# The second statistic of a seam from sums taken before scaling, and seven residual adds on GpSimd during the next products

## Chip, cores and metric

One core of one Trainium2 chip. The metric is the device time of one execution in microseconds (us); lower is better. Three runs of the kernel before are given, and one further execution that was profiled.

## What is computed

The reference is a two-layer backbone over 512 latent tokens and 256 context tokens of width 1024, in float32. Each layer has three sub-layers: a SwiGLU feed-forward, a mixer (state-space heads beside Fourier heads), and another feed-forward. Around each of them stands the same frame:

```python
def _rmsnorm(x, g):
    y = xf * lax.rsqrt(jnp.mean(xf * xf, axis=-1, keepdims=True) + EPS)
    return (y * g.astype(jnp.float32)).astype(x.dtype)
def _pre(x, g, mod, k):
    return _rmsnorm(x, g) * (1.0 + mod[:, 3 * k + 1][:, None]) + mod[:, 3 * k][:, None]
def _post(x, y, g, mod, k, weight):
    return x + weight * mod[:, 3 * k + 2][:, None] * _rmsnorm(y, g)
```

So between two sub-layers the output y of one is normalised, scaled and added to x, and the new x is normalised again and becomes h, the input of the next. I call this stretch a seam. There are five seams between the six sub-layers, and a sixth at the end that only adds to x.

## The kernel before

**Layout.** Activations lie transposed in SBUF: 8 chunks (`KC`) of 128 features in the partitions, with `TOK` = 768 tokens along the row (256 context, 512 latent). `xT` is x, `yT` the output of the sub-layer, `hH` and `hL` the high and low parts of h. From the last mixer's output on only the 512 latent tokens are computed (`tok0` = 256). Each product is three TensorE passes (high by high, low by high, high by low) at L473, over 384 tokens each, or 512 where only latent tokens count. Weights arrive in units of 128x1024; `split_hi` (ScalarE) and `split_lo` (VectorE, L465) part them.

**Order.** Every engine runs one program written out by hand; waits are semaphores. Nothing reorders. Per section the calls are: the sub-layer (`ffn_*` or `mix_*`), then `post_*`, then the `pre_*` part of the next.

**End of a section.** The last eight output chunks are made one after another in `last_chunks` (TensorE), 24 passes each. `last_adds` (VectorE, L992, L1006, L1010) adds each into `yT`; ScalarE squares it into `sq`; GpSimd adds the squares of chunks 0 to 5 up into `sumY` (`add_squares`, L1265). The last two chunks are split in halves of 384 tokens.

**The seam.** TensorE sums `sumY` and the last squares over the features (`row_sums`, L1302); VectorE turns the sums into columns (L1310), ScalarE takes the root (L1376), VectorE the reciprocal (L1462), and TensorE spreads it over all partitions into PSUM (`spread_matmuls`, L1317). Then `post_vector` scales all eight chunks of y (L1471; y from SBUF, the spread row from PSUM). `POOL_CHUNKS`, 0 to 3, are added to x by GpSimd, the others by VectorE (both L1282). ScalarE squares each chunk of the new x (L1411), TensorE sums each (L1302) with filler products between (`keep_clock`, L1326), and the same turn, root, reciprocal and spread follow for x. `pre_vector` makes `tmpN` from x (L1496; x from SBUF, the row from PSUM), ScalarE adds the shift and rounds into `hH` (`add_shift`, L1423), and VectorE makes `hL` from `tmpN` and `hH` (L1500), both in SBUF. Two token ranges, 256 and 512 wide, make two instructions of each per chunk.

**The next section's start.** `first_groups` runs the first weight units together, chunk by chunk as h appears: chunks 0 to 4 for all units, then chunks 5 to 7 unit by unit. A feed-forward opens three units so, a mixer two. A mixer then interleaves projections 2 to 7 with `state_inputs` (L1702), and VectorE scans over the chunks of time (L2105, L2106) beside it; the scans of the first quarter stand behind the split of unit 7, which waits for projection 4. The tile `Tz`, which a DMA loads late in the mixer (waited for at L1764), comes behind the last scan. The mixers and the first feed-forward of each layer store x to DRAM and load it back (`spill_x`, `reload_x`) to use its space.

## Time and profile before

| | us |
|---|---|
| median of three runs | 2648.16 (2646.20 to 2650.08) |
| profiled execution | 2646.27 |
| its span, first to last instruction | 2644.5 |
| TensorE busy | 2586.2 |
| VectorE busy | 1596.0 |
| GpSimd busy | 816.1 |
| ScalarE busy | 714.7 |

The span is one execution; what lies around it is 1.8 us. Busy times overlap, so they do not add up. A seam is read in the chain of waits, which follows the work that ended last back through the engines: the rows below name at each step who was waited for. PE is TensorE, DVE VectorE, ACT ScalarE, POOL GpSimd. In a timeline, instructions of one kind that follow each other are merged; `x15` is their count.

### The profile page before, as it was taken

The page shows a single profiled execution, that of the slowest core. Times are in us where ns is not written, and L with a number is a line of the kernel's source. Part 1 is how long each engine was busy: PE and PEld are TensorE (multiplying, and loading weights), DVE is VectorE, ACT ScalarE, POOL GpSimd, SP SyncE. Part 2 cuts the span into 40 slices and gives each one's busy share as a digit, 9 for nine tenths or more (in the row PEclk, how much of TensorE's full clock was granted, in tenths as well). Part 3 has the DMA queues.
Part 4 walks back from the last instruction along what each step waited for, and adds up shares of the span by engine and source line. Part 5 has one row for each costly group of instructions (what it writes and reads, how often), then busy time and mean ns, then how long its engine had stood idle before and what let it go on. Part 6 is the DMA issues. An engine that isn't in the chain of part 4 may idle for free.

```text
span 2644.5 us, 40750 instructions
## 1 busy us (share of the span) xinstructions
PE 2586.2 (98%) x17044; PEld 2429.9 (92%) x17044; DVE 1596.0 (60%) x2238; ACT 714.7 (27%) x1050; POOL 816.1 (31%) x1286
## 2 busy tenths in 40 slices
PE   6999999999999999999999999999999999999998
PEld 5999999998989899999999899999999878888886
DVE  6688878766574676676676633433343684544443
ACT  4222212123334411212113412122122424322223
POOL 1278876832140100000001148667651131000001
PEclk9999999999999999999999999999999999999999
DMA  9534444453364234434432422222223565233331
GB/s 338 154 123 156 157 143 133 161 187 132 117 194 144 79 98 136 130 108 138 136 104 91 109 67 83 94 92 90 94 88 116 189 196 163 72 96 96 96 96 64
DMA packets 346831, 334.54 MB, mean 127 GB/s; under 512 B 52496, under 2 KB 319896, under 8 KB 343576
## 3 DMA queue, kind: packets, MB, share of 16 engines
q1 hardware_dynamic: 284344, 198.19, 25.7%
q10 hardware_dynamic: 52288, 77.20, 8.7%
q0 software_dynamic: 10016, 56.56, 5.6%
q8 instruction: 134, 2.20, 0.3%
q14 instruction: 49, 0.40, 0.0%
HBM read 287.40 MB, written 44.50 MB: 126 GB/s over the span
## 4 chain that ended last, share of the span: by engine, by line
PE 86%; DVE 8%; POOL 2%; issue 1%; ACT 1%; DMA 1%; SPq 0%; DVEq 0%; POOLq 0%; ACTq 0%
PE ps L473 81%; POOL xT L1282 1%; DVE tmpN L1496 1%; DVE hL L1500 1%; PE ps L1302 1%; PE ps L1317 1%; DVE zb L2105 1%; DVE zd L2106 1%; PE ps L1050 1%; ACT wH L458 1%; PE ps L1069 1%; DVE zc L2118 0%; PE ps L1326 0%; DVE SR L2122 0%; PE ps L1702 0%
## 5 line engine op out<-in xcount | busy, mean ns | idle before, releaser
L473 PE MATMUL ps<-hH,wH 128*128 128x384 f32 (+1 forms) x2928 | 1013.5, 346 | 8.5 <-DVE hL L1500 8.0
L473 PE MATMUL ps<-hH,wL 128*128 128x384 f32 (+1 forms) x2928 | 1004.9, 343 | 0.0
L473 PE MATMUL ps<-hL,wH 128*128 128x384 f32 (+1 forms) x2928 | 1004.5, 343 | 0.0
L465 DVE TENSOR_TENSOR wL<-raw,wH 128x1024 fp32r<-128x1024 f32 x300 | 396.4, 1332 | 493.2 <-ACT wH L458 491.7
L473 PEld LDWEIGHTS ps<-hH,wH 128*128 128x128 f32 x2928 | 549.9, 188 | 35.4 <-DVE hL L1500 7.4
L473 PEld LDWEIGHTS ps<-hH,wL 128*128 128x128 f32 x2928 | 550.1, 188 | 18.1
L473 PEld LDWEIGHTS ps<-hL,wH 128*128 128x128 f32 x2928 | 550.2, 188 | 17.8
L473 PE MATMUL ps<-midH,wH 128*128 128x384 f32 (+1 forms) x1232 | 424.0, 344 | 2.9 <-DVE yT L948 2.5
L473 PE MATMUL ps<-midH,wL 128*128 128x384 f32 (+1 forms) x1232 | 421.5, 342 | 0.0
L473 PE MATMUL ps<-midL,wH 128*128 128x384 f32 (+1 forms) x1232 | 421.3, 342 | 0.0
L458 ACT ACTIVATE wH<-raw 128x1024 fp32r<-128x1024 f32 x300 | 310.9, 1049 | 366.2 <-PE ps L473 349.5
L1265 POOL TENSOR_TENSOR sumY<-sq 128x768 f32<-128x768 f32 (+1 forms) x6 | 10.0, 1659 | 1039.7 <-ACT sq L1384 1039.7
L584 DVE SCALAR_TENSOR_TENSOR adaW<-adaW,siluC 128x384 f32<-128x384 f32 x520 | 329.0, 684 | 0.8
L926 DVE TENSOR_TENSOR midF<-ps,sgate 128x768 f32<-128x768 f32 (+1 forms) x88 | 78.4, 890 | 318.1 <-PE ps L473 317.9
L948 DVE TENSOR_TENSOR yT<-ps,yT 128x768 f32<-128x768 f32 (+1 forms) x256 | 223.2, 885 | 71.3 <-PE ps L473 71.3
L473 PEld LDWEIGHTS ps<-midH,wH 128*128 128x128 f32 x1232 | 231.3, 188 | 13.4 <-DVE yT L948 5.3
L473 PEld LDWEIGHTS ps<-midL,wH 128*128 128x128 f32 x1232 | 231.4, 188 | 6.8
L473 PEld LDWEIGHTS ps<-midH,wL 128*128 128x128 f32 x1232 | 231.3, 188 | 6.8
L882 ACT ACTIVATE midH<-midF 128x768 fp32r<-128x768 f32 (+1 forms) x88 | 69.8, 793 | 575.0 <-DVE midF L926 575.0
L875 ACT ACTIVATE sgate<-ps 128x768 f32<-128x768 f32 (+1 forms) x88 | 66.9, 760 | 216.7 <-PE ps L473 206.1
L930 DVE TENSOR_TENSOR midL<-midF,midH 128x768 fp32r<-128x768 f32 (+1 forms) x88 | 81.8, 930 | 0.0
L666 ACT ACTIVATE modraw<-ps 128x3 f32<-128x3 f32 x76 | 9.1, 172 | 240.7 <-PE ps L473 240.7
(284 smaller groups left out, 2261.3 us busy)
## 6 DMA issues: line engine op xcount, KB each, us to landing
raw<-in_ffn_gu_dram SPq DMA_DIRECT2D x176, 512.0 KB, 3.9
adaW<-in_w_ada_dram ACTq DMA_DIRECT2D x40, 1536.0 KB, 7.0
raw<-in_ffn_down_dram SPq DMA_DIRECT2D x88, 512.0 KB, 3.5
x_d<-xT POOLq DMA_DIRECT2D x4, 3072.0 KB, 11.2
xT<-x_d POOLq DMA_DIRECT2D x4, 3072.0 KB, 10.6
ada_early<-in_w_ada_dram POOLq DMA_DIRECT2D x6, 1536.0 KB, 18.7
W_d<-gW POOLq DMA_DIRECT2D x16, 512.0 KB, 3.8
VT_d<-gVT ACTq DMA_DIRECT2D x16, 512.0 KB, 3.0
```

The source lines that it names most:

```text
L458: nc.scalar.activation(wH[:, n % SPLIT_SLOTS, :], raw[:, n % RAW_SLOTS, :], ACT.Copy).then_inc(w_hi, 1)
L465: nc.vector.tensor_tensor(wL[:, n % SPLIT_SLOTS, :], raw[:, n % RAW_SLOTS, :], wH[:, n % SPLIT_SLOTS, :].bitcast(f32), ALU.subtract).then_ ...
L473: ins = nc.tensor.matmul(dst, a, b, start=first and n == 0, stop=last and n == 3 * len(pairs) - 1)
L584: ins = stt(at, w[:, k], siluC[:, k, v:v + 1], adaP[:] if i == 3 else at, ALU.mult, ALU.add)
L875: nc.scalar.activation(sb_pair(sgate[:, f % 2, :], F.tok0), ps_pair(tile_slot(F, g), F.tok0), ACT.Silu)\
L882: nc.scalar.activation(midH[:, f % 4, F.tok0:TOK], midF[:, f % 2, F.tok0:TOK], ACT.Copy).then_inc(mid_hi, 1)
L926: nc.vector.tensor_tensor(sb_pair(midF[:, f % 2, :], F.tok0), ps_pair(tile_slot(F, g), F.tok0), sb_pair(sgate[:, f % 2, :], F.tok0), ALU.m ...
L930: nc.vector.tensor_tensor(midL[:, f % 4, F.tok0:TOK], midF[:, f % 2, F.tok0:TOK], midH[:, f % 4, F.tok0:TOK].bitcast(f32), ALU.subtract).t ...
L948: ins = nc.vector.tensor_tensor(sb_pair(yT[:, m, :], F.tok0), ps_pair(tile_slot(F, g + m), F.tok0), sb_pair(yT[:, m, :], F.tok0), ALU.add)
L1050: ins = nc.tensor.transpose(ps[:, 6 + a, t * 128:(t + 1) * 128], gV[:, a, t, :], ident[:])
L1069: ins = nc.tensor.matmul(ps[32 * p:32 * p + 32, 6 + g2, c0:c1], Bw[half, a, dd, p, :], rhs(half, a, dd, p), start=first, stop=last)
L1282: engine.tensor_tensor(xT[:, m, N.tok0:TOK], xT[:, m, N.tok0:TOK], yT[:, m, N.tok0:TOK], ALU.add)\
```

## The change

Write z for `coefP`*y, the output times its gate and gain, and r for the reciprocal root of y's mean square. The new x is x + r*z, so its sum of squares is that of the old x, plus 2r times the sum of x*z, plus r^2 times the sum of z^2. The change takes the second statistic from these:

- **Sums of squares per chunk.** `add_squares` is skipped for the five seams with a successor. Instead `square_sums` puts each `sq` chunk through TensorE in `last_chunks`, with `statP` as weights: one column of ones and two of `coefP` squared, so that one pass gives y's sum and those of z for latent and context.
- **Sums of x*z.** `cross_z` (VectorE, in `last_adds`) multiplies yT, `coefP` and xT, chunk by chunk. With 768 tokens chunks 0 to 5 are added up on VectorE, and three row sums are taken behind the last squares; with 512 tokens each chunk has its row sum. x must be back in SBUF by then (`wait_back` moves ahead).
- **The statistic.** `new_sums` (VectorE) has it in five small instructions; a running `sumX` holds the sum of squares of x. `square_x` and the eight row sums of the seam go, with the fillers between.
- **Adds to x.** VectorE adds chunk 0, GpSimd chunks 1 to 7, in the seams with a successor. Before the last output GpSimd keeps four.
- **The seam's order on VectorE.** `joined_vector` scales chunk m+2 of y between `tmpN` and `hL` of chunk m. ScalarE copies the spread row from PSUM to `rowY` in SBUF; chunk 0 is scaled with the row in PSUM, chunks 1 to 7 with `rowY`.
- **Starts.** A mixer opens three units, its state inputs stand one projection later, and the head weights `CW` are made in other banks.

VectorE at the second seam (first mixer to second feed-forward), before: from the last scaling of y to the first low part of h.

```order
L1471 SCALAR_TENSOR_TENSOR yT<-yT,coefP,ps 128x512
L1282 TENSOR_TENSOR xT<-xT,yT 128x768 x4
L465 TENSOR_TENSOR wL<-raw,wH 128x1024
L1310 TENSOR_REDUCE rstdX<-ps 128x6
L1487 RECIPROCAL rstdX<-rstdX 128x6
L1496 SCALAR_TENSOR_TENSOR tmpN<-xT,coefA,ps 128x256
L1496 SCALAR_TENSOR_TENSOR tmpN<-xT,coefA,ps 128x512
L1500 SCALAR_TENSOR_TENSOR hL<-tmpN,coefS,hH 128x256
L1496 SCALAR_TENSOR_TENSOR tmpN<-xT,coefA,ps 128x256
L1500 SCALAR_TENSOR_TENSOR hL<-tmpN,coefS,hH 128x512
```

The same place in the changed kernel, from the scaling of chunk 0 on.

```order
L1582 SCALAR_TENSOR_TENSOR yT<-yT,coefP,ps 128x512
L1632 RECIPROCAL rstdX<-rstdX 128x6
L1347 TENSOR_TENSOR xT<-xT,yT 128x768
L1582 SCALAR_TENSOR_TENSOR yT<-yT,coefP,rowY 128x256
L1582 SCALAR_TENSOR_TENSOR yT<-yT,coefP,rowY 128x512
L1637 SCALAR_TENSOR_TENSOR tmpN<-xT,coefA,ps 128x256
L1637 SCALAR_TENSOR_TENSOR tmpN<-xT,coefA,ps 128x512
L1641 SCALAR_TENSOR_TENSOR hL<-tmpN,coefS,hH 128x256
L1582 SCALAR_TENSOR_TENSOR yT<-yT,coefP,rowY 128x256
L1582 SCALAR_TENSOR_TENSOR yT<-yT,coefP,rowY 128x512
L1641 SCALAR_TENSOR_TENSOR hL<-tmpN,coefS,hH 128x512
L475 TENSOR_TENSOR wL<-raw,wH 128x1024
```

The scalings of chunks 1 to 7 moved from before the second statistic to between `tmpN` and `hL`, and read `rowY`; three of the four adds to x left VectorE.

TensorE at the same seam, before: from the mixer's last product to the first sums over the new x.

```order
L473 MATMUL ps<-hH,wL 128x384
L1302 MATMUL ps<-sumY,ones 32x192 x4
L1302 MATMUL ps<-sq,ones 32x96 x16
L1326 MATMUL ps<-ident 128x128 x3
L1317 MATMUL ps<-ident,rstd 128x128 x6
L1326 MATMUL ps<-ident 128x128 x13
L1302 MATMUL ps<-sq,ones 32x192 x4
L1326 MATMUL ps<-ident 128x128 x3
```

And in the changed kernel, to the next section's first product.

```order
L483 MATMUL ps<-hH,wL 128x384
L1372 MATMUL ps<-sq,statP 32x192 x4
L1372 MATMUL ps<-sq,statP 32x96 x16
L1372 MATMUL ps<-xzM_95,ones 32x192 x4
L1372 MATMUL ps<-xzM_96,ones 32x192 x8
L1388 MATMUL ps<-ident,rstd 128x128 x6
L1397 MATMUL ps<-ident 128x128 x2
L1388 MATMUL ps<-ident,rstdX 128x128 x6
L1397 MATMUL ps<-ident 128x128 x7
L483 MATMUL ps<-hH,wH 128x384
```

The two spreads now follow each other with only fillers between. Not shown: five further row sums of 32x192 stand between the products of the section's last chunks.

```diff
-    def first_groups(pe, base, count, pre, between=None):
-
-        pe.wait_ge(w_lo, base + count)
+    def first_groups(pe, base, count, pre, between=None, cw_ready=None):
+
         lead = KC - 3
         order = [(k, u) for k in range(lead) for u in range(count)]
         order += [(k, u) for u in range(count) for k in range(lead, KC)]
         for k, u in order:
             if u == 0:
                 pe.wait_ge(h_lo, KC * pre.nth + k + 1)
+            if k == 0:
+                pe.wait_ge(w_lo, base + u + 1)
+                if u == 1 and cw_ready:
+                    pe.wait_ge(cw, cw_ready)
+                if u == 2:
+                    pe.wait_ge(row_y, pre.after.nth + 1)
...
+    def cross_sums(pe, S, m):
+
+        pe.wait_ge(cross_x, cross_count(S, m))
+        return row_sums(pe, 6, crossed(S, m), S.tok0, TOK, m == 0, m == KC - 1)
+
+    def square_sums(pe, S, m, t0, t1, first=False, last=False):
+
+        return row_sums(pe, 7, sq[:, m, :], t0, t1, first, last, statP[:, m, :])
...
             signal(last_part(pe, S, m, moving, range(HC), (0, 1)), m)
+            while S.next and m >= 2 and summed < m:
+                pe.wait_ge(sq_y, KC * S.post.nth + summed + 1)
+                square_sums(pe, S, summed, S.tok0, TOK, summed == 0)
+                if S.tok0:
+                    cross_sums(pe, S, summed)
+                summed += 1
...
         if S.next:
             coef_pre(dve, S.next)
+            wait_back(dve, S.post)
+            dlink(dve, nc.vector.memset(statP[:], 1.0))
+            dsync(dve)
+            dlink(dve, nc.vector.tensor_tensor(statP[:, :, 1:3], coefP[:], coefP[:], ALU.mult))
...
             nc.vector.tensor_tensor(at, ps_pair(last_slot(S, m), S.tok0), at, ALU.add).then_inc(S.read, 1)
+            if S.next:
+                dve.wait_ge(S.read, S.read0 + m + 1)
+                ins = cross_z(dve, S, m, token_segments(S.tok0))
+                if S.tok0:
+                    ins.then_inc(cross_x, 1)
+                else:
+                    dlink(dve, ins)
+                    if m:
+                        dsync(dve)
+                        ins = nc.vector.tensor_tensor(crossed(S, 0), crossed(S, 0), crossed(S, m), ALU.add)
+                        if m < CROSS_SUMMED - 1:
+                            dlink(dve, ins)
+                        else:
+                            ins.then_inc(cross_x, 1)
...
-    def add_squares(pool, N):
-
+    def add_squares(pool, N, S):
+
+        if S.next:
+            return
...
-    def post_pool(pool, N):
+    def post_pool(pool, N, S):
         wait_back(pool, N)
-        for m in POOL_CHUNKS:
+        if not N.has_next:
+            for m in range(LAST_POOL):
+                pool.wait_ge(y_norm, KC * N.nth + m + 1)
+                add_to_x(pool, nc.gpsimd, N, m, x_new)
+            return
+        for m in range(1, KC):
             pool.wait_ge(y_norm, KC * N.nth + m + 1)
-            add_to_x(pool, nc.gpsimd, N, m, x_new_pool)
-
-    def row_sums(pe, bank, squares, t0, t1, first, last):
+            add_to_x(pool, nc.gpsimd, N, m, x_new)
...
+            ins = square_sums(pe, S, m, N.tok0 or HALF, TOK, False, m == KC - 1)
+        ins.then_inc(ss_y, 1)
+        for m in range(KC - 3, KC) if N.tok0 else (0, KC - 2, KC - 1):
+            ins = cross_sums(pe, S, m)
+        ins.then_inc(ss_x, 1)
+        pe.wait_ge(rs_y, N.nth + 1)
+        spread_matmuls(pe, 4, 5, N.tok0, rstd, bc_y, bc_y_ctx)
+        keep_clock(pe, 2)
...
+        if S.next:
+            root(act, rstdX[:], sumX[:], N.tok0, sum_x, N.nth + 1, sd_x)
+            act.wait_ge(y_norm, KC * N.nth + 1)
+            for t0, t1, v in token_segments(N.tok0):
+                ins = nc.scalar.activation(rowY[:, t0:t1], seg_ps(4, 5, v), ACT.Copy)
+            ins.then_inc(row_y, 1)
...
+    def scale_y(dve, N, m):
+        for t0, t1, v in token_segments(N.tok0):
+            if m == 0 and v == LAT:
+                dve.wait_ge(bc_y, N.nth + 1)
+            row = seg_ps(4, 5, v) if m == 0 and N.has_next else rowY[:, t0:t1] if N.has_next else seg_ps(2, 3, v)
+            ins = nc.vector.scalar_tensor_tensor(yT[:, m, t0:t1], yT[:, m, t0:t1], coefP[:, m, v:v + 1], row,
+                                                 ALU.mult, ALU.mult)
+        ins.then_inc(y_norm, 1)
+
+    def new_sums(dve, N, S):
+
+        b = N.tok0 // 128
+        r, d, c, x = (t[:, b:6] for t in (rstd, sumD, cross, sumX))
+        dve.wait_ge(rs_y, N.nth + 1)
+        for b0, b1, v in [(b, 2, CTXV), (2, 6, LAT)][b // 2:]:
+            dlink(dve, nc.vector.tensor_tensor(sumD[:, b0:b1], turnedY[:, b0:b1, 1 + v], rstd[:, b0:b1], ALU.mult))
+        dve.wait_ge(ss_x, N.nth + 2)
+        columns(dve, 6, N.tok0, cross).then_inc(cols_x, 1)
+        dve.wait_ge(cols_x, N.nth + 2)
+        dsync(dve)
+        dlink(dve, nc.vector.scalar_tensor_tensor(d, c, 2.0, d, ALU.mult, ALU.add))
+        dsync(dve)
+        dlink(dve, nc.vector.tensor_tensor(d, d, r, ALU.mult))
+        dsync(dve)
+        dlink(dve, nc.vector.tensor_tensor(x, x, d, ALU.add))
+        dsync(dve)
+        nc.vector.tensor_scalar(x, x, 0.0, None, ALU.max).then_inc(sum_x, 1)
...
+    def joined_vector(dve, post, N, late):
+
+        if N.tok0 == 0:
+            dve.wait_ge(bc_y_ctx, post.ctx_nth + 1)
+        dsync(dve)
+        scale_y(dve, post, 0)
+        inverse_x(dve, N)
+        dve.wait_ge(y_norm, KC * post.nth + 1)
+        add_to_x(dve, nc.vector, post, 0, x_new)
+        dve.wait_ge(row_y, post.nth + 1)
+        scale_y(dve, post, 1)
+        dve.wait_ge(bc_x if N.tok0 else bc_x_ctx, N.nth + 1)
+        for m in range(KC):
             if m >= 2:
                 dve.wait_ge(h_lo, KC * N.nth + m - 1)
+            wait_x(dve, post, m)
             for t0, t1, v in token_segments(N.tok0):
-                ins = scaled(m, t0, t1, v)
+                if m == 0 and v == LAT:
+                    dve.wait_ge(bc_x, N.nth + 1)
+                ins = scaled(N, m, t0, t1, v)
+                if m == 0 and v == CTXV:
+                    ins.then_inc(h_tmp_ctx, 1)
             ins.then_inc(h_tmp, 1)
-            if m >= 1:
-                rest(m - 1)
-        rest(KC - 1)
+            if m == 0 and N.tok0 == 0:
+                c, l = token_segments(0)
+                dve.wait_ge(h_hi_ctx, N.nth + 1)
+                low(0, *c)
+                scale_y(dve, post, 2)
+                dve.wait_ge(h_hi, KC * N.nth + 1)
+                low(0, *l).then_inc(h_lo, 1)
+            elif m + 2 < KC:
+                scale_y(dve, post, m + 2)
+                rest(dve, N, m)
+            elif m == KC - 1:
+                rest(dve, N, m - 1)
+                rest(dve, N, m)
+            if m == 0:
+                for n in late:
+                    split_lo(dve, n)
...
-        first_groups(pe, M.base, 2, pre)
+        first_groups(pe, M.base, 3, pre, None, M.gen.n0["cw"] + 1)
```

## Rows read from the trace of the kernel before

**Rows 1.** the page, span and part 1, whole execution: busy us, share, instructions

```profile
...
span 2644.5 us, 40750 instructions
...
PE 2586.2 (98%) x17044; PEld 2429.9 (92%) x17044; DVE 1596.0 (60%) x2238; ACT 714.7 (27%) x1050; POOL 816.1 (31%) x1286
...
```

**Rows 2.** the chain of waits, second seam: start us, us, engine, tile, line

```profile
...
876.15 0.02 issue
...
880.42 0.76 DVE yT L1471
...
881.31 7.16 POOL xT L1282 x4
...
894.30 0.20 DVE rstdX L1487
...
894.55 1.62 PE ps L1317 x12
...
898.63 26.43 PE ps L473 x151
...
```

**Rows 3.** the chain of waits, first seam (two rows), fifth seam (two rows)

```profile
...
635.16 0.02 issue
...
685.77 2.79 PE ps L1702 x64
...
2243.24 0.02 issue
...
2262.26 27.94 PE ps L473 x122
...
```

**Rows 4.** timeline, second seam, VectorE and ScalarE: start us, us, instructions xcount

```profile
...
880.42 8.10 DVE L1471 SCALAR_TENSOR_TENSOR yT<-yT,coefP,ps 128x512 f32<-128x512 f32 x15 [0.41 <-PE ps L1317]
888.43 3.55 DVE L1282 TENSOR_TENSOR xT<-xT,yT 128x768 f32<-128x768 f32 x4
891.90 1.22 DVE L465 TENSOR_TENSOR wL<-raw,wH 128x1024 fp32r<-128x1024 f32 x1
...
903.75 1.14 DVE L1496 SCALAR_TENSOR_TENSOR tmpN<-xT,coefA,ps 128x256 f32<-128x256 f32 x2
904.81 1.14 DVE L1500 SCALAR_TENSOR_TENSOR hL<-tmpN,coefS,hH 128x256 fp32r<-128x256 f32 x2
...
902.69 1.13 ACT L1423 ACTIVATE hH<-tmpN,coefS 128x256 fp32r<-128x256 f32 x2 [1.34 <-DVE tmpN L1496]
...
```

**Rows 5.** timeline, GpSimd and VectorE together; one line's durations, ns, min/median/max

```profile
...
853.13 1.84 POOL L1265 TENSOR_TENSOR sumY<-sq 128x768 f32<-128x768 f32 x1 [46.52 <-ACT sq L1384]
...
854.02 2.03 DVE L465 TENSOR_TENSOR wL<-raw,wH 128x1024 fp32r<-128x1024 f32 x1 [1.86 <-ACT wH L458]
...
L584 DVE SCALAR_TENSOR_TENSOR adaW<-adaW,siluC x520: 602/611/1647, 73.5 to 1417.7; 128x384 f32<-128x384 f32 x174
...
303.01 7.36 DVE L584 SCALAR_TENSOR_TENSOR adaW<-adaW,siluC 128x384 f32<-128x384 f32 x5
...
```

**Rows 6.** TensorE's waits, first mixer and second mixer: us in total, times, longest

```profile
...
PE ps L1764 <- DMA Tz<-strip_d: 0.6, 1, 0.6
...
PE ps L1764 <- DMA Tz<-strip_d: 1.7, 1, 1.7
...
```

**Rows 7.** timeline, TensorE, row sums at the first and the fifth seam

```profile
...
635.08 0.53 PE L1302 MATMUL ps<-sumY,ones 128*32 128x192 f32 x8
635.42 0.68 PE L1302 MATMUL ps<-sq,ones 128*32 128x96 f32 x24
...
2250.46 0.42 PE L1302 MATMUL ps<-sq,ones 128*32 128x128 f32 x8
2250.82 0.94 PE L1326 MATMUL ps<-ident 128*128 128x128 f32 x6
...
```

**Rows 8.** busy us of each engine in two stretches; PEclk is the granted clock

```profile
...
2142.46:2145.07 2.61, 0.01 (x2) 0.03 (x1) 2.58 (x3) 0.24 (x2) 1.32 (x1) 1.00 0.99 377
2145.67:2149.08 3.41, 3.41 (x6) 1.35 (x5) 3.34 (x6) 0.00 (x0) 0.00 (x0) 0.50 1.18 225
...
```

More of the change, by code:

```diff
@@ L1477, in post_vector @@
-        for n in S.late[:1]:
-            split_lo(dve, n)
+        if S.next:
+            new_sums(dve, N, S)
+        else:
+            wait_back(dve, N)
+            dsync(dve)
+            for m in range(KC):
+                scale_y(dve, N, m)
+            for m in range(LAST_POOL, KC):
+                dve.wait_ge(y_norm, KC * N.nth + m + 1)
+                add_to_x(dve, nc.vector, N, m, x_last)
     def flip_rows(dve, N):
         dve.wait_ge(ss_x, N.nth + 1)
-        columns(dve, N.banks[0], N.tok0, rstdX).then_inc(cols_x, 1)
+        columns(dve, N.banks[0], N.tok0, sumX).then_inc(cols_x, 1)
@@ new lines, in scaled, with low, rest @@
+    def scaled(N, m, t0, t1, v):
+        return nc.vector.scalar_tensor_tensor(tmpN[:, m % 2, t0:t1], xT[:, m, t0:t1], coefA[:, m, v:v + 1],
+                                              seg_ps(*N.banks, v), ALU.mult, ALU.mult)
+    def low(m, t0, t1, v):
+        return nc.vector.scalar_tensor_tensor(hL[:, m, t0:t1], tmpN[:, m % 2, t0:t1], coefS[:, m, v:v + 1],
+                                              hH[:, m, t0:t1].bitcast(f32), ALU.add, ALU.subtract)
+    def rest(dve, N, m):
+        dve.wait_ge(h_hi, KC * N.nth + m + 1)
+        for t0, t1, v in token_segments(N.tok0):
+            ins = low(m, t0, t1, v)
+        ins.then_inc(h_lo, 1)
@@ new lines, in first_vector @@
+    def first_vector(dve, N):
+        dve.wait_ge(bc_x_ctx, N.nth + 1)
+        dsync(dve)
+        c, l = token_segments(0)
+        scaled(N, 0, *c).then_inc(h_tmp_ctx, 1)
+        dve.wait_ge(bc_x, N.nth + 1)
+        scaled(N, 0, *l).then_inc(h_tmp, 1)
+        dve.wait_ge(h_hi_ctx, N.nth + 1)
+        low(0, *c)
+        scaled(N, 1, *c)
+        dve.wait_ge(h_hi, KC * N.nth + 1)
+        low(0, *l).then_inc(h_lo, 1)
+        scaled(N, 1, *l).then_inc(h_tmp, 1)
+        for m in range(2, KC):
+            if m in LATE_COEFS:
@@ L1777, in outputs @@
             ins.then_inc(y_ps, 1)
-        for m in range(2, 8):
+        for m in range(3, 8):
             proj(m)
-            if m >= 2 and m < 6:
-                state_inputs(m - 2)
+            if m < 7:
+                state_inputs(m - 3)
         channels(0)
```

214 lines of the change are left out of this document (113 added, 101 removed).

## The prediction

> **What bounds the kernel now.** The page first [rows 1]: TensorE is busy for 98% of the span, and nearly all of it is products at L473, whose number does not change. So only two things can move the time: instructions added to TensorE's stream while it is full, and the stretches at the seams where it has no products. Then the chain of waits through the second seam [rows 2]. The last product ends at 876.15, which I call T. The first product of the next section starts at 898.63, T+22.5. Between lie the first statistic, the scaling of chunk 0 (done at T+5.0), 7.16 us of GpSimd adding four chunks to x, the squares and sums of the second statistic, the second spread of 1.62 us, and the first chunk of h. From 898.63 TensorE is continuous: it has three weight units open, so a chunk of h feeds it for 18 products of 0.175 us (26.43 us over 151), 3.15 us, while VectorE makes a chunk in 2.2. The 24 groups of six end at T+22.5+24 x 1.05 = T+47.7. That moment, three units done over all eight chunks, is what I compare; call it E.
>
> The first seam is the other kind [rows 3]: only two units are open, TensorE follows VectorE, and the third unit is done at 685.77, E = T+50.6; the fourth seam has the same 50.6. The fifth has 512 tokens: products start at T+19.0, a group costs 3 x 0.229 = 0.69, E = T+35.5. The sixth seam keeps its way. Five seams change.
>
> **The change: the seam's head.** The second statistic no longer needs the new x, so GpSimd's 7.16 us and eight squares and sums leave the chain. The start stays: chunk 0 scaled at T+5.0; the three sums of x*z (about 0.4 us each on TensorE, below) lie beside the root and the reciprocal, and the small VectorE operations end before the spread does. I take T+5.1. Then, on VectorE: a reciprocal 0.2, chunk 0 into x 0.9 [rows 4], chunk 1 scaled 1.07: T+7.4; the second spread (1.62 after the reciprocal [rows 2]) is ready by T+7.0, hidden. tmpN of chunk 0 takes 1.14 [rows 4]: T+8.5. So far so good; without anything else the first h would stand near T+10.7.
>
> **The step that decides: GpSimd's adds beside VectorE.** Before, GpSimd's adds ran beside L1471, which reads one operand from PSUM: four adds at 1.79 each while VectorE kept 0.54 per instruction (8.10 over 15) [rows 2, 4]. Nothing waited. Now seven adds run beside instructions that read both operands from SBUF: the scaling of chunks 1 to 7, whose row is now rowY, and hL, from tmpN and hH. What such a pair does is seen where it occurs [rows 5]: L465 begins at 854.02, GpSimd's instruction ends at 854.97, and L465 ends 1.08 after that: 2.03 in place of 1.22. L584, the same kind of instruction as hL, takes 0.61 alone and 7.36 for five in a row beside GpSimd, 1.47 each, one whole GpSimd instruction per VectorE instruction. So the two take turns, an instruction at a time, and I charge each add fully to VectorE unless it falls beside tmpN, which reads PSUM.
>
> Does it fall there? The add of chunk m+2 is released when scaling of m+2 ends. On VectorE the next instructions are the two of hL(m), and only behind them tmpN(m+1). hL waits for ScalarE's 1.13 [rows 4], so GpSimd asks at that very moment, and gets its turn before hL or between its halves. Nothing of it falls beside tmpN. A chunk then costs tmpN 1.14 + scaling 1.08 (two of the 0.54) + hL 1.06 (1.14, begun 0.08 early, row 904.81) + the add 1.82 (row 853.13) = 5.10 us, against 3.15 of TensorE's work.
>
> The Trainium skill, page "SBUF — State Buffer", section "Who interferes with whom", says that a VectorE instruction with two SBUF inputs and a GpSimd instruction that reads SBUF exclude each other for a whole instruction; by it the seams come out at the sum below, without it at that of rival (a). It speaks against the change.
>
> Working it through: the add of chunk 1 (T+7.5 to 9.35) holds back the first half of hL(0); with 0.4, the scaling of chunk 2 1.07 and the second half 0.67, chunk 0 of h is ready at T+11.5. Queued next is one weight split (1.22) behind the add of chunk 2: chunk 1 is ready at 11.5 + 1.82 + 1.22 + 1.14 + 1.07 + 1.07 + 1.82 = T+19.6. Chunks 2 to 5: 4 x 5.10, T+40.0. Chunks 6 and 7 have nothing left to scale: 2 x 2.21, T+44.4. TensorE still owes seven groups then (the units finish one after another over the last three chunks): 0.14 + 7 x 1.05. E = T+51.9.
>
> Against before: second and third seam +4.2 each. First and fourth, where three units are now open: +1.3. But in the first mixer TensorE waits 0.6 for Tz, in the second 1.7 [rows 6], at the end of VectorE's scans; those start from projection 4, ahead of which one block of state inputs less stands now (2.79 [rows 3]), so the scans come 1.5 earlier and the waits absorb: +0.7 and -0.4. Fifth seam, adds of 1.2 to 1.3 (estimate from 1.82 by size), a chunk 3 x 0.67 + 1.28 = 3.3: E between T+32.5 and T+35.8, I take -0.5. **Seams: +8.2.**
>
> **The sections' ends.** While the last eight output chunks run, TensorE is full, and the change puts the sums of squares in there one chunk at a time; the GpSimd additions that it drops there cost nothing (they only made L465 wait, 2.03 against 1.22, with TensorE busy). A row sum of 192 columns is 0.34 from start to start (635.08 to 635.42), its busy time 0.53; one of 128 columns 0.36 with its neighbours [rows 7]. With four interruptions a section I take 0.4 and 0.3: four sections x 5 x 0.4 = 8.0, and the second mixer, which also sums x*z there, 10 x 0.3 = 3.0. **+11.0**, bounds 9 and 14. The new VectorE passes (x*z, and adding it up: about two per chunk of 1 us) lie under 24 x 0.175 = 4.2 us of products per chunk, beside one add and half a split: 3.6 in all. They are free; if the last one slips past T, 0.5 per seam. Moving the head weights costs nothing: ScalarE has time during the stall.
>
> **TensorE's clock.** In the second mixer a gap of 2.61 us was followed by 3.41 us at half clock, 1.2 GHz [rows 8]; gaps up to 1.7 had none. The new seam has gaps of some 5 us between chunks 0 and 1 and of 2 between the others. A slow stretch where TensorE waits anyway costs nothing; on the last seven groups it costs up to 1.7. Bounds 0 and 5 x 1.7; I take one, +1.7. The Trainium skill, page "TensorE: Matmul & The Clock Gate", section "What's actually happening", has the clock fall when the engine has been idle and return with activity; by it each long gap has such a stretch, and the sum would be nearer the upper bound.
>
> Sum: 8.2 + 11.0 + 1.7 = 20.9. The profiled execution took 2646.27 (span 2644.5), the median of the runs is 2648.16, 1.9 more: 2646.3 + 20.9 + 1.9 = **2669 us**.
>
> **Rivals.** (a) The other sign: GpSimd's adds and VectorE's SBUF pairs run side by side after all. A chunk is 3.28, near TensorE's 3.15; chunk 7 is ready at T+32.7, E = T+40.1: -7.6 at two seams, about -11 and -12 at the mixers, -8 at the fifth: -46 + 11 = -35, 2613. It decides from the point where an add costs VectorE under 0.3 us a chunk. For it: L1471 ran undisturbed. Against: [rows 5]. (b) The turns fall kindly: both halves of hL go first and the add lies under tmpN, so that only 0.7 of it is lost. A chunk is 4.0, E = T+46: -17 + 11, 2642; faster or the same by a hair. Against: GpSimd always got the turn after the instruction running. (c) All as forecast, and each seam ends in a slow stretch (4 x 1.7 more) while the row sums reach their bound (+3): 2679. (d) The waits in the mixers do not shrink: +2.3, inside the range, counted with the forecast.
>
> **Numbers.** Forecast 0.57, (a) 0.13, (b) 0.15, (c) 0.15. The range 2638 to 2688 leaves out (a) and a little above (c). About 0.2%, 5.3 us, is what a measurement of this kernel tells from no change. Faster 0.18 (all of (a), a third of (b)), same 0.11 (the rest of (b), a little of the forecast), slower 0.71.
>
> **What the profile would show.** Right: hL and the scaling with rowY near or above 1.1 to 2.5 us an instruction where GpSimd runs, a period near 5.1 us per chunk in the seam, h of chunk 0 near T+11.5 and TensorE idle for about 2 us a chunk, E near T+52. Row sums in the sections' ends lengthening these by about 2 us. Wrong: hL at its 1.07 per chunk throughout, or TensorE continuous after its first new product.

## The result

| | median us | lowest to highest | profiled: time, span |
|---|---|---|---|
| before | 2649.12 | 2646.2 to 2656.12 | 2646.27, 2644.5 |
| changed | 2680.09 | 2676.75 to 2683.55 | 2676.75, 2674.9 |

The changed kernel is slower: a ratio of 1.0112, 95% interval 1.0094 to 1.0130. The forecast was 2669, range 2638 to 2688; the sum was +20.9 and the two profiled spans differ by 30.5 (unrounded). The direction and its main cause came out as predicted; the terms for the sections' ends, the clock and the two mixers were too small.

The page of the changed kernel, span and part 1, against [rows 1]. TensorE executes fewer instructions and idles more; VectorE is busier by 93 us.

```profile
span 2674.9 us, 40386 instructions
...
PE 2568.9 (96%) x16804; PEld 2410.6 (90%) x16804; DVE 1688.7 (63%) x2362; ACT 687.6 (26%) x1019; POOL 800.3 (30%) x1276
```

The chain of waits through the second seam, where T is 883.29 (start us, us, what; against [rows 2]).

```profile
887.16 1.17 DVE yT L1582 x2
...
904.35 0.04 DVE hL L1641
904.38 1.95 issue
906.33 0.74 DVE hL L1641
...
925.37 14.67 PE ps L483 x74
```

Before, TensorE was the chain from T+22.5 on. Now the first product starts at T+11.2, but VectorE stays on the chain until T+42.1, because chunk after chunk stands 1.95 us inside the first of its two hL instructions, in a stretch for which the profile names nobody ("issue"). What happens in those 1.95 us stands in the timeline, VectorE first, then GpSimd (start us, us, then x and the count of instructions).

```profile
903.08 1.14 DVE L1582 SCALAR_TENSOR_TENSOR yT<-yT,coefP,rowY 128x256 f32<-128x256 f32 x2
904.35 2.72 DVE L1641 SCALAR_TENSOR_TENSOR hL<-tmpN,coefS,hH 128x256 fp32r<-128x256 f32 x2
...
904.30 1.83 POOL L1347 TENSOR_TENSOR xT<-xT,yT 128x768 f32<-128x768 f32 x1 [3.13 <-DVE yT L1582]
```

The add into x starts at 904.30, hL at 904.35, and the pair that took 1.14 before [rows 4] takes 2.72. TensorE's longest wait by line, over the whole span (us in total, times, longest), is the one for hL in front of its products:

```profile
PE ps L483 <- DVE hL L1641: 56.6, 33, 3.6
```

The next table says where the 30.5 us are, by the distance from one section's last product to the next; T1 to T5 are the last products ahead of the five seams that change. A section's "end" is the time of the last 192 products before T (96 in the second mixer). E, as in the prediction, is when three weight units are done over all eight chunks, counted from the T in front of it.

| | longer by | of it the section's end | the rest | E before, changed |
|---|---|---|---|---|
| start to T1 | 2.6 | 3.0 | -0.4 | |
| T1 to T2 (first mixer) | 4.5 | 3.1 | +1.5 | 50.6, 52.2 |
| T2 to T3 | 7.6 | 3.1 | +4.5 | 47.7, 52.2 |
| T3 to T4 | 7.5 | 3.1 | +4.4 | 47.7, 52.2 |
| T4 to T5 (second mixer) | 7.8 | 3.8 | +4.0 | 50.6, 52.3 |
| T5 to the end | 0.4 | | +0.4 | 35.7, 35.3 |

So 16.1 us lie in the ends and 14.4 in the seams and what follows them. Ratios below are to the kernel before, with their 95% interval; the changed kernel's is the 1.0112 above. The kernel before was run again beside each group of experiments, with medians from 2649 to 2655, so small steps are better read from the ratios than from the medians.

### The profile page after: what moved, and what is told of

Read it like the earlier page. It is cut to its first block, busy times and chain, and to the rows that moved or that the text cites. A ratio compares the mean times of both kernels' runs of the same rounds, so it can differ in the third digit from the quotient of the medians.

```text
span 2674.9 us, 40386 instructions
## 1 busy us (share of the span) xinstructions
PE 2568.9 (96%) x16804; PEld 2410.6 (90%) x16804; DVE 1688.7 (63%) x2362; ACT 687.6 (26%) x1019; POOL 800.3 (30%) x1276
## 4 chain that ended last, share of the span: by engine, by line
PE 80%; DVE 11%; issue 3%; ACT 2%; DMA 1%; POOL 1%; SPq 1%; DVEq 0%; ACTq 0%; POOLq 0%
PE ps L483 77%; DVE tmpN L1637 1%; DVE hL L1641 1%; DVE yT L1582 1%; ACT hH L1543 1%; DVE wL L475 1%; PE ps L1372 1%; DVE zb L2282 1%; DVE zd L2283 1%; POOL xT L1347 1%; PE ps L1111 1%; SPq L1754 1%; PE ps L1130 1%; ACT wH L468 0%; DVE zc L2295 0%
## 5 line engine op out<-in xcount | busy, mean ns | idle before, releaser
L1347 POOL TENSOR_TENSOR xT<-xT,yT 128x768 f32<-128x768 f32 (+1 forms) x39 | 67.1, 1724 | 910.1 <-DVE yT L1582 910.1
L1641 DVE SCALAR_TENSOR_TENSOR hL<-tmpN,coefS,hH 128x256 fp32r<-128x256 f32 (+1 forms) x88 | 91.4, 1074 | 4.2
## 6 DMA issues: line engine op xcount, KB each, us to landing
xT<-x_d POOLq DMA_DIRECT2D x4, 3072.0 KB, 11.5
```

The costliest lines, as they stand in the source:

```text
L1347: engine.tensor_tensor(xT[:, m, N.tok0:TOK], xT[:, m, N.tok0:TOK], yT[:, m, N.tok0:TOK], ALU.add)\
L1641: return nc.vector.scalar_tensor_tensor(hL[:, m, t0:t1], tmpN[:, m % 2, t0:t1], coefS[:, m, v:v + 1], hH[:, m, t0:t1].bitcast(f32), ALU.ad ...
```

## Experiments

### The adds on VectorE, and no adds

```diff
     def post_pool(pool, N, S):
...
-        for m in range(1, KC):
-            pool.wait_ge(y_norm, KC * N.nth + m + 1)
-            add_to_x(pool, nc.gpsimd, N, m, x_new)
     def joined_vector(dve, post, N, late):
...
+            if m + 1 < KC:
+                dve.wait_ge(y_norm, KC * post.nth + m + 2)
+                add_to_x(dve, nc.vector, post, m + 1, x_new)
```

> The changed kernel, with the seven additions into x of each seam on VectorE (behind hL of the chunk before) and none on GpSimd. Theory (the two engines take turns, and an add costs VectorE its whole 1.8 us): a chunk becomes tmpN 1.14 + scaling 1.08 + hL 1.1 + add 0.96 = 4.3 us in place of 4.95, chunk 0 of h is ready 0.4 earlier, and E (three units done over all chunks) falls from T+52.1 to about T+46; over four seams about -20 us, so 2658 to 2662. Rival (GpSimd does not hold VectorE back, and the period of 4.95 comes from VectorE's own instructions with two SBUF operands): every chunk gets 0.96 longer, a period near 5.9, E near T+58, and the kernel is some 20 us slower than the changed one, near 2700.

Measured: 2672.49 us, ratio 1.0074 (1.0057 to 1.0091). The rival falls: the kernel became faster than the changed one, not 20 us slower. But the gain is 10 by the ratios (8 by the medians), not 20. The second kernel leaves out the adds into x of chunks 1 to 7, so it gives a price and is no candidate.

> The changed kernel without the additions into x of chunks 1 to 7 of the five seams (that part of the computation is left out; chunk 0 is still added). It prices them. Theory (turns): hL takes its 1.1 us and the period falls from 4.95 to 3.3, near TensorE's 3.15; chunk 0 of h is ready near T+10.7, E near T+40; four seams by 12 and some 2 at the fifth, less what waits for Tz and for state inputs give back in the mixers: 2680 - 40 = 2640, and 2630 to 2655 as bounds. Rival (a mere part of the 4.95 is the adds, the rest ScalarE's hH on the way): the period stays above 4, E above T+46, 2660 or more.

Measured: 2635.18 us, ratio 0.9935 (0.9919 to 0.9951). The timelines of VectorE, first without adds, then with the adds on VectorE:

```profile
1466.90 1.15 DVE L1640 SCALAR_TENSOR_TENSOR hL<-tmpN,coefS,hH 128x256 fp32r<-128x256 f32 x2
1467.96 1.13 DVE L1636 SCALAR_TENSOR_TENSOR tmpN<-xT,coefA,ps 128x256 f32<-128x256 f32 x2
...
1471.36 1.13 DVE L1636 SCALAR_TENSOR_TENSOR tmpN<-xT,coefA,ps 128x256 f32<-128x256 f32 x2
```

```profile
908.70 1.15 DVE L1638 SCALAR_TENSOR_TENSOR hL<-tmpN,coefS,hH 128x256 fp32r<-128x256 f32 x2
909.77 0.95 DVE L1347 TENSOR_TENSOR xT<-xT,yT 128x768 f32<-128x768 f32 x1
```

Without adds the forecast held (2640, period 3.3, E T+40): hL is back at 1.15 and a chunk takes 3.39 (1467.96 to 1471.36); E falls to T+40.4 in two seams and T+42.0 in the others. In the changed kernel a chunk takes 4.95, so one add of 1.80 on GpSimd costs VectorE 1.56. On VectorE itself it costs 0.95 and 0.1 until tmpN follows: 4.45 per chunk, half a microsecond less than 4.95, where I had expected 4.3. E falls to T+48.9 (49.7 at the first seam), not 46, and the two full seams give 3.3 each. The first mixer, however, became 5.2 us longer from T to T, although its E came 2.6 earlier. TensorE's waits there, which were 0.2 and nothing in the changed kernel:

```profile
PE ps L1944 <- DMA Tz<-strip_d: 3.0, 1, 3.0
PE ps L1882 <- ACT ZI L2105: 2.1, 1, 2.1
```

Neither wait is for an instruction of VectorE; they pointed at the queue of the next experiment. The spans differ by 1.9 only, but this profiled execution was the longest of its four (2674.76), and its first mixer had a further slow stretch of TensorE's clock, so the median says more.

### SyncE's queue in the mixers

```diff
-        load_units(RAW_SLOTS, 5)
+        load_units(RAW_SLOTS, 6)
         sp.wait_ge(h_lo, KC * pre.nth + KC)
         load_phases(1)
+        load_units(6, 7)
         load_chunks(0)
+        load_units(7, 8)
         load_chunks(1)
-        load_units(5, 7)
...
-        load_units(7, 8)
```

> The changed kernel with SyncE's queue in the mixers in another order: the loads of weight units 5, 6 and 7 stand ahead of the loads of the projected chunks 0, 0 and 1 instead of behind chunk 1 and behind the first state inputs. Theory (in the changed kernel these loads wait in the queue behind loads that wait for projections and state inputs one projection later than before, so ScalarE waits 14.7 us for them in the second mixer and comes late to the state inputs): ScalarE's wait falls to some 3 us, TensorE's wait of 2.5 us for the state inputs' buffer goes, and the second mixer gets 2.5 to 4 us shorter, the first 0 to 1.5: 2680 - 4 = 2676. Rival (the wait comes from the state inputs themselves standing one projection later, with the loads beside the path): ScalarE's wait may shrink but TensorE's 2.5 us stay, no change within 0.1%.

Measured: 2674.10 us, ratio 1.0082 (1.0066 to 1.0098); 2676 was expected. The interval still touches that of the changed kernel (1.0094 to 1.0130), so the evidence is in the traces. The second mixer, T to T, is 3.8 shorter (201.8 against 205.6); the first is 1.4 shorter, as much as its E came earlier (T+50.9). The changed kernel's chain of waits there shows the cause: SyncE issues the small loads of the projected chunks one at a time, 0.43 and 0.04 each, sixteen in a row (2121.11 to 2128.82), and the weights behind them arrive late, so that ScalarE reaches the state inputs (ZI) late.

```profile
...
2128.39 0.43 SPq L1754
2128.82 0.04 issue
2128.87 4.41 DMA raw<-in_w_in_dram
...
2137.31 1.75 ACT ZI L2105 x6
```

SyncE's timeline in the same mixer, changed kernel, then the experiment (T is the same within 0.1): the loads of units 5 and 6 went out at T+61.2 (T+50.7 in the kernel before) and that of unit 7 at T+69.0; now unit 5 stands ahead of this stretch, unit 6 goes at T+50.0 and unit 7 at T+56.2.

```profile
2128.87 1.06 SPq L459 DMA_DIRECT2D raw<-in_w_in_dram  x2
...
2136.66 0.56 SPq L459 DMA_DIRECT2D raw<-in_w_in_dram  x1
```

```profile
2117.58 0.37 SPq L459 DMA_DIRECT2D raw<-in_w_in_dram  x1
...
2123.78 0.49 SPq L459 DMA_DIRECT2D raw<-in_w_in_dram  x1
```

And TensorE's waits over that mixer, changed kernel and experiment. The wait for ZI is gone, and most of the one for Tz.

```profile
PE ps L1927 <- DMA ctxCS<-in_dft_ctx_dram: 2.6, 1, 2.6
PE ps L1882 <- ACT ZI L2105: 2.5, 1, 2.5
PE ps L1944 <- DMA Tz<-strip_d: 1.5, 1, 1.5
```

```profile
PE ps L1927 <- DMA ctxCS<-in_dft_ctx_dram: 2.6, 1, 2.6
...
PE ps L1944 <- DMA Tz<-strip_d: 0.4, 1, 0.4
```

### The row sums behind the last product

```diff
             signal(last_part(pe, S, m, moving, range(HC), (0, 1)), m)
-            while S.next and m >= 2 and summed < m:
-                pe.wait_ge(sq_y, KC * S.post.nth + summed + 1)
-                square_sums(pe, S, summed, S.tok0, TOK, summed == 0)
-                if S.tok0:
-                    cross_sums(pe, S, summed)
-                summed += 1
...
-        square_sums(pe, S, KC - 3, N.tok0, TOK)
+        for m in range(KC - 2):
+            square_sums(pe, S, m, N.tok0, TOK, m == 0)
```

> The changed kernel with the row sums of squares of chunks 0 to 4 (and in the second mixer those of x*z) behind the section's last product instead of between the last chunks' products. Theory (a row sum costs 0.61 us there because it interrupts the stream of products; side by side they cost 0.34 each): the last 192 products take 33.9 us again in place of 37, 3.1 less in each of four sections and 3.8 in the second mixer; behind T five more sums of 0.34 stand ahead of the last squares, where 0.25 us was idle, +1.45 in each seam. Net -1.6 in four sections and about -2.4 in the fifth: -9, 2671. Rival (0.61 is the price of the row sum itself wherever it stands): +2.8 behind T against -3.1 before it, about -2 in all, 2678.

Measured: 2673.01 us, ratio 1.0077 (1.0060 to 1.0093), 9 us below the changed kernel by the ratios and 7 by the medians; 9 was expected. The ends are back at 33.9, 34.2, 33.8, 33.4 and 22.0, within 0.05 of before, and the first product comes only 1.16 later. So the row sums are all that had made the ends longer. The profiled span fell by 3.7 only: the experiment's TensorE spent more time at the lower clock (granted clock 0.986 in all four executions, 0.988 to 0.991 in the changed kernel), among it a stretch of 10.2 us late in the second mixer that the changed kernel's trace does not have. In the changed kernel, two row sums together between products, and one alone (TensorE's timeline):

```profile
859.35 0.86 PE L1372 MATMUL ps<-sq,statP 128*32 128x192 f32 x16
860.14 0.44 PE L483 MATMUL ps<-hH,wH 128*128 128x384 f32 x1
...
864.23 0.34 PE L483 MATMUL ps<-hH,wL 128*128 128x384 f32 x1
864.50 0.53 PE L1372 MATMUL ps<-sq,statP 128*32 128x192 f32 x8
864.96 0.45 PE L483 MATMUL ps<-hH,wH 128*128 128x384 f32 x1
865.25 0.34 PE L483 MATMUL ps<-hL,wH 128*128 128x384 f32 x1
```

Products start 0.17 apart. With one row sum between them it is 0.73, and 0.29 to the next product in place of 0.17: 0.67 in all. A second row sum beside the first adds 0.33 (0.79 from 859.35 to 860.14, against 0.46 from 864.50 to 864.96). So 0.33 is the row sum itself, and about as much, 0.34, goes into the change from products to row sums and back. Four such changes and five row sums are 3.0; measured 3.06, or 0.61 per row sum. Behind T, in the experiment (the next row is the sums of x*z), and the place in the changed kernel where TensorE waits for the last squares:

```profile
881.95 2.82 PE L1365 MATMUL ps<-sq,statP 128*32 128x192 f32 x80
884.59 1.16 PE L1365 MATMUL ps<-xzM,ones 128*32 128x192 f32 x24
```

```profile
884.50 0.37 PE L1372 MATMUL ps<-sq,statP 128*32 128x96 f32 x8 [0.25 <-ACT sq L1515]
```

The sums of x*z begin 2.57 after T (882.02) and began 1.40 after T in the changed kernel, 1.17 for five row sums. They take 5 x 0.33 = 1.65 there, and some 0.5 of it falls into the wait for the last squares, so 0.23 each is what they add behind T and not what a row sum costs. The price of the change is that of another shape of product: the products are 128*128 and the row sums 128*32, and eight products of another kind but the same shape, in the stream of the changed kernel, cost nothing beyond their own 0.11 each (two products that start 0.17 apart stand 0.97 apart around them, and 0.26 to the next: 0.88 for the eight).

```profile
342.38 1.04 PE L1111 MATMUL ps<-ident,gV 128*128 128x128 f32 x8
```

The Trainium skill, page "TensorEngine Tiling (Array Packing)", section "Key Properties", says that a change of tiling mode drains TensorE; the rows agree, with 0.34 for the change there and back.

### Another order on VectorE

```diff
-            elif m + 2 < KC:
-                scale_y(dve, post, m + 2)
-                rest(dve, N, m)
...
+        for m in range(1, KC):
+            if m + 1 < KC:
+                product(m + 1)
+            rest(dve, N, m)
+            if m + 3 < KC:
+                scale_y(dve, post, m + 3)
```

`product` is the two `scaled` of a chunk (tmpN) with their waits, `rest` is hL.

> The changed kernel with another order on VectorE in the seam: behind the scaling of chunk m+3 now comes tmpN of chunk m+2, which reads PSUM, and only then hL of chunk m+1; nothing else moves, GpSimd still adds. Theory (an add costs VectorE only what of it does not lie beside an instruction with a PSUM operand): of the 1.80 of an add 1.1 lie beside tmpN and 0.7 hold hL back, so a chunk takes 3.39 (the period without adds) + 0.7 = 4.1 in place of 4.95; E at the second and third seam T+47 to T+48 in place of T+52.1, the mixers gain less because SyncE's queue holds their weight loads back: 2680 - 12 = 2668, bounds 2662 and 2673. Rival (the price of an add is the same 1.56 wherever it lies, by load on the memory rather than by turns): period 4.95 again, E T+52, 2680.

Measured: 2652.58 us, ratio 1.0000 (0.9989 to 1.0011), below the expected bound of 2662: the whole loss of the change is undone by the order of three instructions. GpSimd's add now starts under tmpN:

```profile
1481.04 1.13 DVE L1637 SCALAR_TENSOR_TENSOR tmpN<-xT,coefA,ps 128x256 f32<-128x256 f32 x2
1482.09 1.90 DVE L1641 SCALAR_TENSOR_TENSOR hL<-tmpN,coefS,hH 128x256 fp32r<-128x256 f32 x2
...
1484.97 1.13 DVE L1637 SCALAR_TENSOR_TENSOR tmpN<-xT,coefA,ps 128x256 f32<-128x256 f32 x2
...
1481.20 1.84 POOL L1347 TENSOR_TENSOR xT<-xT,yT 128x768 f32<-128x768 f32 x1 [2.08 <-DVE yT L1582]
```

The add is as long as ever, tmpN is not touched (1.13), hL loses 0.75 in place of 1.56, and a chunk takes 3.93. E is T+45.6 (44.5 at the second seam). The gain is 28 by the medians and 30 by the ratios, more than twice the 12 that I had expected. Per section: -7.7 and -6.6 behind the two full seams, -3.2 and -3.3 in the mixers, -3.6 behind the fifth. E came 2 us earlier than worked out, as a chunk took 3.93, not 4.1, and no slow stretch of TensorE's clock lay on the last groups any more; and I had counted nothing for the fifth seam. The mixers still waited for ZI, 1.9 and 4.8 us: SyncE's queue again.

### The row in PSUM, and all together

For the scaling of all chunks the row stays in PSUM, and GpSimd's add is released by an hL, so that it runs beside the scaling and tmpN. Not shown are the new order on VectorE and the later start of the third weight unit, which the expectation describes.

```diff
-            row = seg_ps(4, 5, v) if m == 0 and N.has_next else rowY[:, t0:t1] if N.has_next else seg_ps(2, 3, v)
+            row = seg_ps(4, 5, v) if N.has_next else seg_ps(2, 3, v)
...
         for m in range(1, KC):
             pool.wait_ge(y_norm, KC * N.nth + m + 1)
+            if m >= 2:
+                pool.wait_ge(h_lo, KC * S.next.nth + m - 1)
```

> The changed kernel with the row of the scaling left in PSUM for all chunks, the order scaling (chunk m+3), tmpN (m+1), hL (m), and GpSimd's add of chunk m+2 released by hL of chunk m-1, so that it runs beside scaling and tmpN, which both read PSUM; the third weight unit waits for the last scaling (its banks) and makes up its first five chunks then. Theory (turns): hL takes 1.15 a chunk again and nothing is held back, period 3.4 as without adds; the third unit starts near T+28, E T+42 to T+44; in the mixers SyncE's queue takes back what goes beyond T+49: near 2680 - 2 x 9 - 2 x 3 = 2656, bounds 2648 and 2668. Rival (the price of an add does not depend on where its neighbour's operand lies): period 4.95, the third unit starts near T+36, E near T+52, 2680.

Measured: 2669.19 us, ratio 1.0062 (1.0041 to 1.0082). The mechanism held and the kernel did not: I had released the add one hL too late, and tmpN waited for it, a period of 4.29 and E at T+47.7 to T+48.9. The next kernel puts the row in PSUM, the row sums behind T and the reordered queue together.

```profile
1486.20 1.14 DVE L1638 SCALAR_TENSOR_TENSOR tmpN<-xT,coefA,ps 128x256 f32<-128x256 f32 x2 [1.02 <-POOL xT L1350]
1487.26 1.14 DVE L1642 SCALAR_TENSOR_TENSOR hL<-tmpN,coefS,hH 128x256 fp32r<-128x256 f32 x2
```

> The changed kernel with the PSUM row and its order, the row sums behind the last product, and SyncE's weight loads ahead of the chunks' loads in the mixers, together. If the three causes are separate and add up: seams E T+43 to T+45 (1.2 later for the row sums) against 52.1, four times, is -32; sections' ends -3.1 x 4 - 3.8 = -16; the second mixer's state inputs -3: 2680 - 48 = 2632, bounds 2625 and 2645, under the kernel before by 0.6%. If the mixers stay bound by SyncE's queue instead, their E does not count, and it comes out 10 to 14 later, near 2645, no different from the kernel before.

Measured: 2647.92 us, ratio 0.9983 (0.9973 to 0.9994), above the upper bound of 2645, with the late release still in it (E T+48.9, 50.0 at the second seam). Against the PSUM row alone that is -21 us by medians: the two mixers, T to T, came to 239.8 and 194.9 against 245.5 and 205.3 (their ends' 3.1 and 3.8 among it). With `if m >= 3: ... m - 2` in the release:

> The kernel with the three changes together, its GpSimd adds released one hL earlier (by hL of chunk m-3). In the run with all three an add was released so late that VectorE waited 0.9 for it in every chunk, a period of 4.29 with hL at 1.15. Theory (turns, adds free beside instructions with a PSUM operand): period 3.4, E near T+44 (it was T+48.9), the third unit from T+28 on, 5 us off at each of four seams, of which the mixers keep at least half: 2647 - 15 = 2632, bounds 2626 and 2638. Rival (an add costs something even beside PSUM operands, 0.5 or more a chunk): period 3.9 or more, E T+47, 2640 or more.

Measured: 2630.00 us, ratio 0.9926 (0.9909 to 0.9943). VectorE and GpSimd in the third seam:

```profile
1469.49 1.13 DVE L1577 SCALAR_TENSOR_TENSOR yT<-yT,coefP,ps 128x256 f32<-128x256 f32 x2
1470.54 1.13 DVE L1632 SCALAR_TENSOR_TENSOR tmpN<-xT,coefA,ps 128x256 f32<-128x256 f32 x2
1471.59 1.14 DVE L1636 SCALAR_TENSOR_TENSOR hL<-tmpN,coefS,hH 128x256 fp32r<-128x256 f32 x2
1472.64 1.13 DVE L1577 SCALAR_TENSOR_TENSOR yT<-yT,coefP,ps 128x256 f32<-128x256 f32 x2
...
1469.71 1.83 POOL L1343 TENSOR_TENSOR xT<-xT,yT 128x768 f32<-128x768 f32 x1 [4.38 <-DVE hL L1636]
```

An add of 1.83 stands beside two pairs with a PSUM operand, and none of them, nor hL behind them, is longer than alone. A chunk takes 3.15 (1469.49 to 1472.64). The rival, that an add costs something everywhere, falls. E was T+46.4 all the same, not T+44; the next section says why. The last kernel of this group has the other order with `rowY` in place of the PSUM row, again with the row sums behind T and the reordered queue.

> The changed kernel with the other order on VectorE (tmpN behind the scaling), the row sums behind the last product, and SyncE's weight loads ahead in the mixers. The order alone measured E T+45.6, ratio 1.000, and kept waits of 1.9 and 4.8 for the state inputs' buffer in the mixers, which the earlier loads should take away (they did with the changed kernel's order); the row sums alone gave 9. If they add up: 2652.5 - 6.7 - 9 = 2637, bounds 2631 and 2643, a ratio near 0.994 to the kernel before. If the mixers' waits come from something other than the queue: 2643.

Measured: 2633.33 us, ratio 0.9936 (0.9921 to 0.9951), 4 us better than expected. The mixers' waits of 1.9 and 4.8 for ZI are gone, as the queue theory wants.

### What bounds E now

With the PSUM row TensorE stood 5.4 us between chunks 0 and 1, where VectorE had a weight split, both operands in SBUF, beside GpSimd's add of chunk 2:

```profile
1463.87 2.54 DVE L475 TENSOR_TENSOR wL<-raw,wH 128x1024 fp32r<-128x1024 f32 x1
```

```diff
         product(1)
-        for n in late:
-            split_lo(dve, n)
+        if N.tok0:
+            for n in late:
+                split_lo(dve, n)
         for m in range(1, KC):
...
             rest(dve, N, m)
+            if m == 1 and N.tok0 == 0:
+                for n in late:
+                    split_lo(dve, n)
```

> The kernel with the PSUM row and the adds released in time, and the split of the third weight unit behind hL of chunk 1 instead of ahead of the scaling of chunk 4 (that unit is used from T+30 on only). In the run before, that split stood at T+14.2 beside a GpSimd add and took 2.54, chunk 1 of h came at T+19.9, and TensorE stood 5.4 between chunks 0 and 1. Theory (this gap is VectorE's queue, and E is now TensorE's own work plus its gaps): chunk 1 2.5 to 2.8 earlier, the gap near 2.7, E near T+44 in place of T+46.4, -2.5 at two seams and up to that at the other two: 2630 - 8 = 2622, bounds 2619 and 2628. Rival (the later split and adds give the time back at chunks 2 to 4, or the third unit starts later by as much): E T+46, 2630.

Measured: 2623.91 us, ratio 0.9885 (0.9869 to 0.9902), 1.1% under the kernel before. The split takes 1.21 in its new place, as GpSimd is idle when it starts; now GpSimd's add, which starts 0.23 behind the split, is the longer one (2.69 in place of 1.83). E came to T+45.0; I had expected T+44. By the spans of the two profiled executions the step is worth 4.3, by the ratios 0.4%, with intervals that just miss each other.

```profile
1463.94 1.21 DVE L475 TENSOR_TENSOR wL<-raw,wH 128x1024 fp32r<-128x1024 f32 x1
```

This kernel keeps the idea of the change (the second statistic from sums of x*z and z squared) and wins by what was put around it. From T to T the two mixers are 6.2 and 7.4 shorter than before, the two full seams with their sections 2.6 and 2.7. The reordered queue was not tried on the kernel before, so its share in this is not shown; TensorE waited 0.6 and 1.7 for Tz there [rows 6].

## Why the prediction held, and where it did not

**The seam's head was right.** Chunk 0 was scaled at T+5.0 (predicted 5.1), and chunk 0 of h was ready at T+11.1 (11.5).

**The deciding step was right in kind; that E came out at 52.2 against 51.9 is partly luck.** I charged each chunk 3.28 of VectorE's own work and the whole add of 1.82: 5.10. Measured: 3.39 of its own, as hL starts 0.13 behind the scaling, when ScalarE's hH is ready, and 1.56 for the add, both from the run without adds. That is 4.95 in all. Chunk 1 came 0.8 earlier than worked out and chunk 5 1.4 earlier, at T+38.6. VectorE then makes tmpN of chunks 6 and 7 and only then their hL, so that chunk 6 stood at T+42.1 and chunk 7 at T+43.1, not 44.4. TensorE owed eight groups from T+42.1 on, 8.4 us, and one slow stretch of its clock fell on them, 1.7: E T+52.2. The prediction had no slow stretch in its E of 51.9 (the clock is a term of its own there), so chunks that came 1.4 too early and a stretch of 1.7 cancelled. That the two take turns, and that only instructions with both operands in SBUF are held, is shown by four kernels: no add (hL 1.15), the add half under tmpN (1.90), fully under PSUM readers (1.14), and in front of hL (2.72). Beside the add tmpN kept its 1.13, in the other order and with the PSUM row. The Trainium skill, page "SBUF — State Buffer", section "Who interferes with whom", has it so; the trace agrees in kind, and what an add of 1.80 cost VectorE here was 1.56.

**Rival (b) described a better kernel.** Its period of 4.0 and E of T+46 are what the other order gives (3.93, T+45.6); this order does not give them, since the add asks just before hL.

**The first and fourth seam: a step that failed.** I let the mixers' waits for Tz absorb part of it, from scans that come 1.5 earlier: +0.7 and -0.4. Measured +1.5 and +4.0. The scans did not come earlier: from T they began 1.1 later than before in the first mixer and 4.8 later in the second. The waits for Tz shrank only to 0.2 and 1.5, nearly rival (d), and in the second mixer the wait of 2.5 for ZI was new. I had moved the state inputs behind one more projection and priced only TensorE's instructions; SyncE's queue holds 16 small loads of the projected chunks ahead of the weights of units 5 and 6, and they moved too. With these loads reordered the scans of the second mixer began 1.3 earlier than before the change, and the mixer gave 3.8 back.

**The sections' ends: the mis-sized term.** +11.0 predicted with bounds 9 and 14, +16.1 measured: 0.61 per row sum in place of 0.4. The ten sums in the second mixer cost 0.38 each in place of 0.3. The 0.34 of [rows 7] is the row sum beside another, and it was right (0.33); what I gave for the change of shape, 0.06, was too little. The price stood in the trace of the kernel before, where row sums stand between the filler products of the second seam:

```profile
890.31 0.53 PE L1302 MATMUL ps<-sq,ones 128*32 128x192 f32 x8
890.77 0.49 PE L1326 MATMUL ps<-ident 128*128 128x128 f32 x2
891.19 0.53 PE L1302 MATMUL ps<-sq,ones 128*32 128x192 f32 x8
```

From one row sum to the next it is 0.88, and a filler takes 0.11 (six take 0.94 and two 0.49), so the row sum with its changes costs 0.66. The 0.36 that I had read in [rows 7] runs from the row sum's start to the fillers' start, and leaves out what the changes cost outside these two. VectorE's new passes were free, as said: with the row sums gone from them, the ends were as long as before.

**The clock.** I took one slow stretch on the last groups, for all seams together; it came at four of the five. The windows of the second seam's two stretches (PEclk is the granted clock; 0.50 is 1.2 GHz), and the same length of time behind the second one:

```profile
902.09:905.50 3.41, 3.34 (x10) 3.34 (x11) 3.28 (x6) 1.12 (x2) 1.20 (x1) 0.50 0.00 0
...
925.99:929.40 3.41, 3.41 (x13) 3.41 (x12) 0.87 (x4) 1.55 (x2) 0.00 (x0) 0.50 0.54 82
929.40:932.81 3.41, 3.41 (x22) 3.41 (x21) 1.59 (x2) 1.49 (x2) 0.00 (x0) 1.00 1.06 394
```

The first lies where TensorE waits for chunks anyway. The second, behind four gaps of 1.9 to 2.4 from one product's start to the next, lies in the last eight groups: 13 products in place of 22, which is the 1.7 of the prediction, four times. It was booked as rival (c), at 0.15, and belonged to the forecast: (c) has 2679, and 2680 was measured, though its row sums are too cheap still and it leaves the mixers out. The Trainium skill, page "TensorE: Matmul & The Clock Gate", section "What's actually happening", has the clock fall when the engine has been idle and return with activity; the trace agrees, and the sum nearer the upper bound, which the prediction derived from that page, was the better one.

**Fifth seam:** E came 0.3 earlier (0.5 predicted), right, and T5 to the last section's last product is 0.3 shorter. What follows that product is 0.8 longer, where a slow stretch of the clock is twice as long (6.8 against 3.4).

The sum, measured against predicted: mixers 5.5 against 0.3, the two full seams 8.9 against 8.4, from T5 to the end 0.4 against -0.5, the start -0.4 against 0, a clock term of 1.7 that is contained in these, ends 16.1 against 11.0. That is 5.2 + 0.5 + 0.9 - 0.4 - 1.7 + 5.1 = 9.6, from 20.9 to 30.5.

## What to carry to other kernels

Work given to GpSimd to relieve VectorE was free only beside VectorE instructions that read one operand from PSUM. Look at which instruction is queued at the moment when the GpSimd work is released, and move the PSUM reader there; here that order alone was worth 1.1%.

Small row sums cost least side by side and where TensorE waits, and twice that (0.67 against 0.33) one at a time in a full stream. To price such an insertion, measure from the work before it to the work behind it, with both changes inside. When a step moves, follow what it issues into every queue behind it, SyncE's above all.

## What the hardware showed that was not expected

- One add of 1.80 on GpSimd costs VectorE 1.56 when it starts just ahead of hL; the same add with 0.9 of it under tmpN costs 0.75 (hL 1.90 against 1.15), and under two PSUM readers nothing.
- A row sum of 192 columns costs TensorE 0.67 alone between products and 0.33 behind another; the 0.34 between is the change of shape there and back. Eight products of 128 columns in the same shape as their neighbours cost 0.88, nothing beyond their own time.
- SyncE issues most of the small loads of the projected chunks 0.47 us apart, and sixteen hold the queue for 7.7 us.
- The turns bind both engines: an add on GpSimd that starts 0.23 behind VectorE's weight split takes 2.69 in place of 1.83, and a split that starts beside an add takes 2.54 in place of 1.21.
- Slow stretches move from run to run. In the run with the reordered queue the first seam's second stretch began at T+40.7 and E was T+50.9; in the changed kernel it began at T+42.5 and E was T+52.2, with the same work in between.
